# One block of a diffusion transformer on one core: heads of a pair alternate on TensorE, and the first weight pieces go out ahead of the modulation rows

## The reference

```python
sh1, sc1, g1, sh2, sc2, g2 = modulation(c, ada_w, ada_b)      # silu(c) @ ada_w + ada_b
zl = (xl * (1 + sc1) + sh1) @ w_in                            # the same for the context: zc
yc_l = neighbourhood_attention(q, k, v, k_ctx, v_ctx, rpb)    # 12 heads of 64
# per head: softmax over [window keys + bias, all 256 context keys], then times the values
mix_l = concat([ya_l, yb_l, yc_l]) @ w_out                    # gMLP, RWKV-7 scans, attention
xl = layer_norm(ALPHA * xl + g1 * mix_l)
xl = layer_norm(ALPHA * xl + g2 * sq_relu_mlp(xl * (1 + sc2) + sh2))
```

## Time and profile before

| | before |
|---|---|
| median of 3 runs (lowest to highest) | 3442.66 us (3437.31 to 3445.47) |
| profiled execution: time | 3433.65 us |
| profiled execution: span on the core | 3431.9 us |
| mean granted TensorE clock | 0.953 |
| busy: PE, DVE, ACT, POOL | 92%, 45%, 22%, 31% |
| first 640 us | rows, three tiles, attention |

### The profile page before, as it was taken

One profiled execution on the slowest core, in us unless ns is written; L12 is line 12 of the kernel. 1 busy time (PEld: TensorE's weight loads), 2 busy tenths in 40 slices (PEclk: granted clock), 3 DMA queues, 4 the chain that ended last, 5 costly groups with the idle time before them and its releaser, 6 DMA issues.

```text
span 3431.9 us, 70492 instructions
## 1 busy us (share of the span) xinstructions
PE 3166.9 (92%) x30308; PEld 2619.3 (76%) x30308; DVE 1552.5 (45%) x1999; ACT 747.1 (22%) x1103; POOL 1051.2 (31%) x482
## 2 busy tenths in 40 slices
PE   6599999999997599999969899999999999999996
PEld 0477777777775599999958778888888888888885
DVE  0666556335767344544442273334333333343335
ACT  0212222102222222222221232222222222222221
POOL 0233334434331000000004444444444444444442
PEclk7799999999998799999979999999999999999998
DMA  9665455322322311011042222222222222222222
GB/s 405 226 224 198 167 169 192 118 76 76 129 96 112 146 42 35 30 48 45 14 172 94 96 68 98 92 98 92 98 92 97 94 96 95 94 97 93 98 92 110
DMA packets 96802, 387.40 MB, mean 113 GB/s; under 512 B 10816, under 2 KB 11840, under 8 KB 90048
## 3 DMA queue, kind: packets, MB, share of 16 engines
q1 hardware_dynamic: 74400, 297.84, 24.7%
q10 hardware_dynamic: 21888, 84.03, 6.9%
q0 software_dynamic: 288, 2.10, 0.2%
HBM read 352.73 MB, written 31.20 MB: 112 GB/s over the span
## 4 chain that ended last, share of the span: by engine, by line
PE 87%; DMA 6%; DVE 5%; issue 1%; ACT 1%; SPq 0%; POOL 0%; ACTq 0%; DVEq 0%; POOLq 0%
PE bank L862 15%; PE bank L863 15%; PE bank L864 15%; PE bank L619 11%; PE bank L510 6%; PE bank L511 6%; PE bank L512 6%; DMA buf<-ada 2%; PE bank L635 1%; DMA buf<-adarows 1%; PE bank L812 1%; PE bank L695 1%; PE bank L794 1%; DMA buf<-small_lncol 1%; PE bank L795 1%
## 5 line engine op out<-in xcount | busy, mean ns | idle before, releaser
L486 POOL TENSOR_TENSOR buf<-buf 128x1024 fp32r<-128x1024 f32 x288 | 696.9, 2420 | 1625.6 <-ACT buf L1230 1625.6
L862 PE MATMUL bank<-buf 128*128 128x512 f32 x2304 | 904.1, 392 | 19.2 <-DVE buf L1664 18.7
L863 PE MATMUL bank<-buf 128*128 128x512 f32 x2304 | 903.4, 392 | 0.0
L864 PE MATMUL bank<-buf 128*128 128x512 f32 x2304 | 903.4, 392 | 0.0
L1230 ACT CAST buf<-buf 128x1024 fp32r<-128x1024 f32 x288 | 302.5, 1050 | 1254.0 <-PE bank L864 1252.8
L862 PEld LDWEIGHTS bank<-buf 128*128 128x128 f32 x2304 | 432.9, 188 | 117.5 <-issue 20.4
L864 PEld LDWEIGHTS bank<-buf 128*128 128x128 f32 x2304 | 432.8, 188 | 97.2
L863 PEld LDWEIGHTS bank<-buf 128*128 128x128 f32 x2304 | 433.0, 188 | 96.8
L619 PE MATMUL bank<-buf 64*64 64x64 f32 x13248 | 426.2, 219 | 50.4 <-DMA buf<-scaled_receptances 30.6
L510 PE MATMUL bank<-buf 128*128 128x512 f32 (+1 forms) x1168 | 436.9, 374 | 38.8 <-POOL buf L480 36.1
L619 PEld LDWEIGHTS bank<-buf 64*64 64x64 f32 x13248 | 409.9, 136 | 62.6 <-DMA buf<-scaled_receptances 31.9
(11 more groups left out here) (215 smaller groups left out, 2499.0 us busy)
## 6 DMA issues: line engine op xcount, KB each, us to landing
buf<-stream SPq DMA_DIRECT2D x382, 512.0 KB, 3.2
buf<-adarows ACTq DMA_DIRECT2D x92, 512.0 KB, 4.8
buf<-ada SPq DMA_DIRECT2D x32, 1024.0 KB, 13.1
buf<-adarows SPq DMA_DIRECT2D x36, 512.0 KB, 6.2
scaled_keys<-buf ACTq DMA_DIRECT2D x18, 768.0 KB, 5.1
buf<-scaled_keys SPq DMA_DIRECT2D x18, 768.0 KB, 6.5
buf<-tokens SPq DMA_DIRECT2D x4, 1536.0 KB, 21.1
buf<-bias ACTq DMA_DIRECT2D x6, 1024.0 KB, 5.2
```

Source lines behind the costliest of these rows:

```text
L486: G.tensor_tensor(wl2[b % SPLIT2], raw2[b], wh2[b % SPLIT2].bitcast(F32), ALU.subtract).then_inc(split2, 1)
L862: pe.matmul(bank[:, :], lh, rh, start=start, stop=False)
L863: pe.matmul(bank[:, :], lh, rl, start=False, stop=False)
L864: return pe.matmul(bank[:, :], ll, rh, start=False, stop=stop)
```

## The change

Three things. On TensorE attention goes block by block: `scores(b)` makes the window scores of both heads, then the context scores of both; `values(b)` alternates between the heads within each of its four parts. The head h = 0 uses partitions 0 to 63 and h = 1 partitions 64 to 127 of queries and keys, and columns 0 to 63 and 64 to 127 of the values. Per block there are `scores(b)`, `turn(2b-2)`, three projection steps, `turn(2b-1)`, three steps, `values(b-1)`. On SP pieces 2 and 3 go ahead of row 0, piece 4 ahead of row 4, and pieces 5, 6 and 7 ahead of rows 6, 11 and 16. ScalarE takes a projection tile at x = 2 and 6 ahead of `turned(x-1)` and not behind it. Vector's and GpSimd's programs stay as they are.

```diff
+            early = {0: 2, RINGR: 1, RINGR + 2: 1, RINGR + 7: 1, RINGR + 12: 1}
+            pieces = RINGW
             for n in range(2 * KT + RINGR):
-                half_row(sp, n)
-                if n >= RINGR and n % 5 == 0 and pieces < RINGW + 6:
+                for _ in range(early.get(n, 0)):
                     piece(pieces)
                     pieces += 1
+                half_row(sp, n)
...
-            def scores(x):
-                b, h = divmod(x, 2)
-                hs = slice(64 * h, 64 * h + 64)
-                if x >= 2:
-                    w("sadd", x - 1)
-                qt = qs[hs, P * b:P * b + P]
-                pe.matmul(Q[x % 2][:, 0:256], qt, kv[hs, :, WIN0[b]:WIN0[b] + WC], start=True, stop=True)
-                pe.matmul(Q[x % 2][:, 256:512], qt, ks[hs, 0:CTX], start=True, stop=True).then_inc(C["smm"], 1)
+            heads = [slice(64 * h, 64 * h + 64) for h in range(2)]
+
+            def scores(b):
+                if b:
+                    w("sadd", 2 * b)
+                queries = [qs[hs, P * b:P * b + P] for hs in heads]
+                for h, hs in enumerate(heads):
+                    pe.matmul(Q[h][:, 0:256], queries[h], kv[hs, :, WIN0[b]:WIN0[b] + WC], start=True, stop=True)
+                for h, hs in enumerate(heads):
+                    pe.matmul(Q[h][:, 256:512], queries[h], ks[hs, 0:CTX], start=True, stop=True).then_inc(C["smm"], 1)
...
-            def values(x):
-                b, h = divmod(x, 2)
-                w("tpe", x + 1)
+            def values(b):
+                w("tpe", 2 * b + 2)
                 for c in range(4):
-                    src = vw[:, 2 * b + c if c < 2 else 6 + c, 64 * h:64 * h + 64]
-                    mm = pe.matmul(Q[4][64 * h:64 * h + 64, P * b:P * b + P], src, PT[x % 2][:, c, :],
-                                   start=c == 0, stop=c == 3)
-                mm.then_inc(C["pv"], 1)
-
-            for x in range(10):
-                if x < 8:
-                    scores(x)
-                    advance(nxt, 2)
-                if 1 <= x < 9:
-                    turn(x - 1)
-                    advance(nxt, 1)
-                if x >= 2:
-                    values(x - 2)
+                    for h, hs in enumerate(heads):
+                        mm = pe.matmul(Q[4][hs, P * b:P * b + P], vw[:, 2 * b + c if c < 2 else 6 + c, hs], PT[h][:, c, :],
+                                       start=c == 0, stop=c == 3)
+                        if c == 3:
+                            mm.then_inc(C["pv"], 1)
+
+            for b in range(5):
+                if b < 4:
+                    scores(b)
+                if b:
+                    turn(2 * b - 2)
+                advance(nxt, 3)
+                if b:
+                    turn(2 * b - 1)
+                advance(nxt, 3)
+                if b:
+                    values(b - 1)
             finish(nxt)
...
             for x in range(9):
                 if x < 8:
                     expo(x)
+                if x in (2, 6):
+                    act_take_tile(act, 3 * t.j + 3 + x // 4, x // 4)
                 if x >= 1:
                     turned(x - 1)
...
-                if x in (2, 6):
-                    act_take_tile(act, 3 * t.j + 3 + x // 4, x // 4)
```

More of the change, by code:

```diff
@@ L412, in _ @@
                 sp.dma_start(raw[b], stream1[b]).then_inc(rawld[b], 16)
-            pieces = RINGW
             def piece(n):
```

## The result

The changed kernel takes 3461.44 us, the median of 4 runs (3457.17 to 3465.61). The kernel before, run beside it on the same chip, takes 3440.23 us (4 runs, 3437.31 to 3445.47). The ratio is 1.0057 (95% interval 1.0041 to 1.0074): the change costs 21.2 us, against a forecast of 5.7 us gained.

A forecast was written before the change was run, and what follows sets the result against it. TensorE paced pairs 0 to 4 before; after the change vector was to set a pair's end. Savings of 2.5 + 2 + 1.2 = 5.7 us from the 3442.66 us median gave 3437 us, range 3408 to 3456.

The forecast's parts named there:

- pairs 0 to 4: Attention of the first five head pairs: 0.5 us saved in each, 2.5 us together.
- pair 5: Last head pair, already bound by vector: one wait less for scores per block, 2 us saved, between 0 and 5.
- front, until pair 0's transposes: Row stage and modulation sum ahead of attention, with pieces moved early: net 1.2 us saved, between -2 and +3.
- the layout of vector in a pair: Vector's steps, rows and waits from a pair's first score: head 7's normalisation ends at 48.7 us and sets the pair's end.
- The GpSimd term: Vector's rows in a pair slowed beside GpSimd's splitting of pieces: 5.2 us, between 3 and 10.
- the landing term: Vector waiting for modulation rows to land: 3.5 us in block 1, some 1.2 us each in blocks 2 and 3.
- The tail: Pair's end: values end at 51.4 us, after normalisation at 48.7; TensorE idles, then loses 2.6 us to the low clock.
- The rival that ends slower: Vector's lateness outweighs pairing: normalisation at 51 us, 1.4 to 2.5 us lost a pair, 3451 to 3457; slower case 0.28.
- Two pieces fewer: Row stage ahead of attention: four pieces beside it for six, saving 4.0 to 9.8 us, taken as 7.5.
- the products overlap: Alternating heads on TensorE: a block's scores take 0.88 us for 2.10, values 0.97 for 2.04; 9.1 us a pair.
- the row wait in block 1: Second block of a pair: vector wants rows at 12.3 us, they land at 15.8, so it waits 3.5 us.
- The rival "products don't overlap": TensorE keeps 54.9 us of work a pair plus an idle tail: 10 to 15 us slower; within slower case, 0.28.

## Why the prediction was wrong

Forecast were 3437 us in a range of 3408 to 3456; measured are 3461.44. The sum had three terms, and each came out on the other side (measured between the two profiled executions):

| term | forecast | measured |
|---|---|---|
| pairs 0 to 4 | -2.5 us | +16.8 us |
| pair 5 | -2 us | +1.4 us |
| front, until pair 0's transposes | -1.2 us | +3.0 us |
| sum | -5.7 us | +21.2 us |

**The step that failed is the layout of vector in a pair**: "the last normalisation (head 7) thus ends at ... 48.7 us". In pair 1 it ends at 53.1 us after the first score (339.24 less 286.13). By its own terms:

- Start and idle time of block 0: 1.2 + 3.75 us, forecast 1.0 + 3.5. Right.
- Waits for landing: 4.71 + 0.51 + 2.19 = 7.4 us, forecast 3.5 + 2.4 = 5.9.
- GpSimd: (5.40 + 3.45 + 4.57 - 3 x 2.47) + 0.07 + (2.15 - 0.49) = 7.7 us, forecast 5.2 with a range of 3 to 10.
- Steps and rows at their undisturbed lengths: 33.1 us, as forecast.

The GpSimd term is off by 2.5 us and the landing term by 1.5, together nearly all of the 4.4 us between 53.1 and 48.7; nothing new had to be found for either. The kernel with early rows gives back 7.2 us (45.9), as much as the landing term measured. The kernel with the narrow subtraction gives back 5.0 of the 7.7 us (48.1), while 1.9 us more go into waiting for rows.

**The tail was right in kind and a little short.** Forecast: 2.7 us from the last normalisation to the end of the values. Measured: 3.7, as the values themselves already ran at the lower level, 1.97 us for 1.0. Forecast 2.6 us for the clock; measured 1.0 in the values and 1.4 behind them (342.98 to 355.63 for 335.7 to 346.90 before). Tail and clock together are 5.1 us, forecast 5.3. So a pair that should have gained 0.5 us lost 3.4, and the 3.9 between them are the 4.4 of the normalisation, less 0.2 here and 0.4 that I had set aside for gaps. The 3.4 us are also the mean of pairs 0 to 4 (16.8 / 5), and 3.9 times five is all of the 19 us between forecast and measurement there. That the other four pairs lose it in the same way isn't shown.

**The rival that ends slower named the mechanism.** It put the last normalisation at 51 us and said that the case turns at about 50. The runs bear this out:

| kernel | last normalisation after the first score | pair 1 against before |
|---|---|---|
| changed | 53.1 us | +3.4 us |
| narrow subtraction | 48.1 us | -1.4 us |
| rows issued first | 45.9 us | -6.5 us |
| before | | 0 (68.8 us) |

Between the first two a straight line crosses zero at 49.6 us, an estimate from two executions. But that rival lost 1.4 to 2.5 us a pair where 3.4 were lost, and its total stopped at 14 us. The range ended there, at 3456, because I took the worst value of one term and not of both: all rows disturbed and late landing together.

**The front**: the first row was forecast at 138.1 and came at 138.04. "Two pieces fewer save 4.0 to 9.8 us; I take 7.5" came out at 4.4 us: the 32 rows took 64.5 us (138.04 to 202.57) instead of 61.4. I had priced only vector's time. In that stage vector waits 17.3 us for rows to land, in 14 waits, and before it waited 18.8 in 14. So landing sets part of the pace (the DMA share is 0.85 in both), and less work beside vector is worth only part of its length. The second miss is the clock: after 21 us of idling the sum took 6.96 us, not 5.10. (The 0.8 us forecast for slower transposes belongs to pair 0 in the table above; they took 2.37 us.) The kernel with the pieces alone has the same 6.96, and the one with the old pieces 4.07.

**Pair 5**: the 2 us that I took for one wait less per block weren't there. I didn't take this pair apart; its loss is 1.4 us, and what failed there stays open.

**Right**: the products overlap (scores 1.06 us a block for 0.88 forecast, values 1.02 for 0.97), which is 8.2 us a pair for 9.1. Both heads' values share a bank at 1.02 us. The rule of the Trainium skill that I weighed (TensorEngine Tiling (Array Packing), section Restrictions and Gotchas) is about row tiles in one bank; the values are column tiles, and no run here puts two row tiles into one bank. Right too were the row wait in block 1, the wait of turn(7) for vector, and the slow clock behind it. The rival "products don't overlap" is out. One reading of the trace of before was loose: the pair of rows at 266.00 starts ahead of the subtraction (266.62) and loses 2.5 us to it (4.95 less 2.47), not the 3.3 of its length.

**Still open**: why the loss per pair spreads from 0.9 us (pair 2) to 5.2 us (pair 4). Each pair meets GpSimd's pieces at other points, and two executions of kernels with equal medians differ by 2 us in a pair, but I only took pair 1 apart. And the experiments don't add up to a budget: removing late rows, row work or GpSimd's work gives 39, 31 and 34 us, each more than the whole loss. All three shorten the one chain that vector runs, and no kernel here tells how much of each gain is the same gain.

## What to carry to other kernels

When products of an engine that sets the pace are bunched, ask what else hung on the old rhythm. Here the rows were issued behind a copy that waited for a turned head; the loads had arrived in time only because a head came every 7 us, and the early issue alone turned 0.6% slower into 0.6% faster. And when a slower chain is about to become the last, price all its disturbances at their bad ends together before setting the range, since they fall on one sum.

## What the runs showed of the hardware

- Products of different rows of the array overlapped when they were merely next to each other. Two heads' scores without alternating took 1.07 us a block, alternating 1.06, and 2.10 us (twice 1.05) with other work between them. For value products, which differ in columns, the order did matter: 1.51 us in runs, 1.02 alternating, 2.04 (twice 1.02) apart. The Trainium skill, TensorE: Matmul & The Clock Gate, Part 3, says that a weight load overlaps with products in flight only where its rows differ. The scores agree with it. The values share all their rows and gain all the same, so for them the word "only" isn't borne out.
- Of the clock: 4.42 us of idling ahead of turn(7) left TensorE at 1.2 GHz for some 7 us (339.29 until about 346.1; granted clock 0.50). After 21.01 us of idling 32 one-column products took 6.96 us, against 3.63 us at 2.4 GHz.
- Vector's normalisation, with SBUF as its only source, took 2.15 us for 0.49 when it met GpSimd. The Trainium skill, SBUF — State Buffer, section SBUF: two separate sides, has whichever comes second wait out a whole instruction of the other. The 5.40 us pair (2.9 us more than 2.47) agrees: its second row, started at 305.75, ends at 309.13, about one row's length behind GpSimd's subtraction (304.83 to 308.05).
